# Attention scores of a query tile's two jobs made as one run of matmuls

## The chip, the cores and the metric

One core of a Trainium2 chip runs the whole program. The metric is device microseconds of an execution. TensorE (PE; its weight loads are shown as PEld) makes the matmuls and transposes into PSUM, VectorE (DVE) and ScalarE (ACT) read PSUM and work on SBUF, GpSimd (POOL) works on SBUF, SyncE (SP) issues most DMAs. Each engine runs its own instructions in the order of the program and waits on semaphores.

## The reference

A block of a language model with 1024 tokens: projections, retention, a sparse attention with three branches, two feed-forward layers and a recurrent mixer. The change touches two of the attention's branches, for 8 heads of 64 in 2 key groups:

```python
ss = jnp.einsum('bgrtd,bgtnsd->bgrtns', qb, kb).astype(jnp.float32) * scale
ss = jnp.where(dsel >= 0, ss - sl[..., None, None] * dsel, NEG)
ps = jax.nn.softmax(ss.reshape(B, G, R, T, -1), axis=-1).reshape(ss.shape)      # selected blocks
...
wmask = (dw >= 0) & (dw < WINDOW) & (wpos[None, :] >= 0)
sw = jnp.where(wmask, sw - sl[..., None] * dw.astype(jnp.float32), NEG)
pw = jax.nn.softmax(sw, axis=-1)                                               # the last 512 keys
...
o = gt[0] * o_cmp + gt[1] * o_sel + gt[2] * o_win
```

## The kernel before

The function `nsa_attend` works through 128 jobs, `JOBS = [(h, i, r) ...]`: head h (8), query tile i of 128 tokens (8), and r = 0 for the selected branch, r = 1 for the window. Job j = 2n + r; the two jobs of one (h, i) are a pair, number n. The selected job of tile i has i + 1 key tiles of 128 (causal; what isn't selected is masked by rows that stand with the keys), the window job at most 5.

A job goes through five steps, each on one engine:

- scores (PE): for each run of up to 512 keys a matmul of the queries' low part with the keys and mask rows (`q_low`, 82 rows, `ks_blk` or `kw_blk`), one of the high part with both parts of the keys (`q_high`, `ks_both` or `kw_both`), accumulating in the PSUM tile `sc0` or `sc1` (one for each r, 1024 columns); then a matmul with `eye` and `edges` that adds the causal mask to the last tile, and for window jobs with 5 tiles one for the first tile. The last one counts up `scores_done{r}`.
- maxima (DVE, L2237) and exp with the row sum (ACT, L2220), which writes `att_prob{r}` and counts up `exp_done{r}`. From here the PSUM tile is free for the next pair's scores of the same r.
- weight (DVE, L2246 to L2251): reciprocal of the sum, times the gate, and the scaling of `att_prob`.
- turns (PE, L2170): a transpose for each key tile, into `pt0` or `pt1` in groups of up to 4 tiles; groups with even numbers are copied to SBUF by ACT (L2227), odd ones by DVE (L2273).
- values (PE, L2187): the products with the values, both jobs of a pair into one PSUM tile; the selected job's step begins with two matmuls (L2183) that add the earlier branch's output. After the window job's values, output (DVE, L2261 and L2262) splits the sum into two parts.

The order is written out by hand, one loop over j on each engine. PE: scores(0), scores(1), then for each j scores(j + 2), turns(j), values(j - 1). DVE: for each j weight(j + 1), maxima(j + 2), the odd copies of job j, output(j - 1), which does nothing unless j - 1 is a window job. ACT: for each j the even copies of job j, then exp(j + 2). So scores(j + 2) wait for exp(j), the job of the same r one pair before.

POOL splits each head's queries into `q_high` and `q_low` (L1997 to L1999, four operations), for heads 2 to 7 as soon as the last scores of the head before the last are done, that is, while the last tile of one head and the first of the next are worked on.

Of the kernel before, what the change touches and what calls it, by code (L numbers as in the profile page):

```python
# [6 lines left out]
P = 128  # L7
# [10 lines left out]
HALF = 512  # L18
# [11 lines left out]
NSA_H, NSA_G, NSA_D = 8, 2, 64  # L30
# [3 lines left out]
N_KROWS = N_BLK + 2  # L34
WINDOW = 512
# [2039 lines left out]
def nsa_attend(nc, mem, env, N, projT, selT, ocmp, then, ins):  # L2075
# [8 lines left out]
    qh, q_high, q_low = N["qh"], N["q_high"], N["q_low"]  # L2084
# [7 lines left out]
    JOBS = [(h, i, r) for h in range(NSA_H) for i in range(NT) for r in range(2)]  # L2092
    NJ, PER_HEAD = len(JOBS), 2 * NT
    first = lambda i, r: 0 if r == 0 else max(0, i - WINDOW // P)
    tiles = lambda i, r: i + 1 - first(i, r)
# [8 lines left out]
    with phase(nc, names, banks) as (block, s, ps):  # L2104
        def groups_of(j, parity=None):
            return [n for n in range(before[j], before[j + 1]) if parity is None or n % 2 == parity]

        @block.sync
        def _(sp):
            sp.dma_start(raw, then).then_inc(s["weight_loaded"], 16)  # L2110
            for h in range(1, NSA_H):
                p, b = divmod(h, 2)
                before_it = p - 1 + b
                if before_it > 0:
                    sp.wait_ge(s[f"q_split{b}"], before_it)
                load_queries(nc, sp, qh[b], projT, selT, ins, h, s[f"q_in{b}"])
                if h == 1:
                    for i in range(NT):
                        sp.dma_start(N["o"][:, i, :], ocmp[:, i, :]).then_inc(s[f"o_in{i}"], 16)
# [19 lines left out]

        @block.tensor  # L2140
        def _(pe):
            def scores(j):
                h, i, r = JOBS[j]
                p, b = divmod(h, 2)
                if i == 0 and h > 0:
                    pe.wait_ge(s[f"q_split{b}"], p + b)
                pe.wait_ge(s[f"exp_done{r}"], j // 2)
                n, f, rows = tiles(i, r) * P, first(i, r) * P, NSA_D + N_KROWS
                both_parts, high = (N["ks_both"], N["ks_blk"]) if r == 0 else (N["kw_both"], N["kw_blk"])
                q = slice(i * P, (i + 1) * P)  # L2150
                for c in range(0, n, HALF):
                    w = min(HALF, n - c)
                    out, k = ps[f"sc{r}"][:, c:c + w], slice(f + c, f + c + w)
                    edge, diagonal = n > WINDOW and r == 1 and c == 0, c + w == n
                    nc.tensor.matmul(out, q_low[b][0:rows, q], high[0:rows, p // 2, k], start=True, stop=False, skip_group_check=True)
                    last = nc.tensor.matmul(out, q_high[b][:, q], both_parts[:, p // 2, k], start=False, stop=not (edge or diagonal), skip_group_check=True)
                    if edge:
                        last = nc.tensor.matmul(out[:, 0:P], N["eye"][:], N["edges"][:, P:2 * P], start=False, stop=True, skip_group_check=True)
                    if diagonal:
                        last = nc.tensor.matmul(out[:, w - P:w], N["eye"][:], N["edges"][:, 0:P], start=False, stop=True, skip_group_check=True)  # L2160
                last.then_inc(s[f"scores_done{r}"], 1)

            def turns(j):
                r = JOBS[j][2]
                pe.wait_ge(s[f"scaled{r}"], j // 2 + 1)
                for n in groups_of(j):
                    _, t0, nt = GROUPS[n]
                    pe.wait_ge(s[f"group_copied{n % 2}"], n // 2)
                    for t in range(nt):
                        last = nc.tensor.transpose(ps[f"pt{n % 2}"][:, t * P:(t + 1) * P], prob[r][:, (t0 + t) * P:(t0 + t + 1) * P], ident[:])  # L2170
                    last.then_inc(s[f"grouped{n % 2}"], 1)

            def values(j):
                h, i, r = JOBS[j]
                p, b = divmod(h, 2)
                for n in groups_of(j):
                    pe.wait_ge(s[f"group_copied{n % 2}"], n // 2 + 1)
                out = ps[f"ob{i % 2}"][b * NSA_D:(b + 1) * NSA_D, 0:P]
                if r == 0:
                    if h == 0:  # L2180
                        pe.wait_ge(s[f"o_in{i}"], 16)
                    pe.wait_ge(s[f"o_read{i % 2}"], h * (NT // 2) + i // 2)
                    nc.tensor.matmul(out, N["o"][:, i, h * NSA_D:(h + 1) * NSA_D], ident[:], start=True, stop=False)  # L2183
                v = N["vs"] if r == 0 else N["vw"]
                cols = slice(p // 2 * NSA_D, (p // 2 + 1) * NSA_D)
                for t in range(tiles(i, r)):
                    last = nc.tensor.matmul(out, v[:, first(i, r) + t, cols], probT[r][:, t, :],  # L2187
                                            start=False, stop=(r == 1 and t == tiles(i, r) - 1))
                last.then_inc(s[f"o_done{r}"], 1)

            scores(0)
            scores(1)
            for j in range(NJ):
                if j + 2 < NJ:
                    scores(j + 2)
                turns(j)
                if j > 0:
                    values(j - 1)
            values(NJ - 1)
# [1555 lines left out]
```

## Time and profile before

| | |
|---|---|
| median of 3 runs | 3888.74 us (3884.55 to 3891.54) |
| the profiled execution | 3891.31 us, its span 3889.5 us |
| mean granted TensorE clock | 0.943 of full speed |
| busy: PE, PEld, DVE, ACT, POOL | 90%, 74%, 46%, 22%, 27% of the span |
| attention stage (`nsa_attend`) | 917.9 us (first scores) to 1288.5 us (first matmul of the next stage): 371 us |

Busy shares are means over stages with different limits. The times of the trace count from the start of the span; 1.8 us of the profiled execution lie outside of it.

### The profile page before, as it was taken

Reading aid. Unit: us, or ns where it says so; the run is one execution under the profiler, and the core shown is the slowest. Engines: PE = TensorE matmul, PEld = TensorE weight load, DVE = VectorE, ACT = ScalarE, POOL = GpSimd, SP = SyncE. Lnnn points to the kernel's source line nnn. Section 1 sums busy time; section 2 is a strip of 40 time slices with the busy share of each in tenths; the row PEclk is TensorE's granted clock in tenths of the full one; section 3 lists DMA queues with packets and bytes.
Section 4 is the critical chain, followed back from the end, with each engine's and each line's share of the span. In section 5 each row is a group of like instructions: output and inputs, shape, how many; then the busy total and the mean of one; then the engine's idle time right before and its main releaser. Section 6 shows DMA issues by size and latency. Waiting matters only on the chain. (4 is left out here: it accounts for less than half of the span.)

```text
span 3889.5 us, 55742 instructions
## 1 busy us (share of the span) xinstructions
PE 3510.9 (90%) x23201; PEld 2896.4 (74%) x23201; DVE 1777.2 (46%) x2725; ACT 868.9 (22%) x1258; POOL 1032.2 (27%) x491
## 2 busy tenths in 40 slices
PE   5999999988989889999999789688874889999997
PEld 4878777767777777888888678577763778888886
DVE  4752555324777635555555535144433322323233
ACT  2012122122334212111111220244322131111112
POOL 3333333333110333212212144132202332222121
PEclk7999999999999999999999899889886999999998
DMA  3353433342000312322222164200002111111111
GB/s 97 130 177 115 124 102 109 103 123 81 8 5 1 128 44 76 119 87 73 88 70 81 44 168 120 82 19 34 5 3 94 51 50 40 58 38 59 38 49 44
DMA packets 309559, 285.55 MB, mean 73 GB/s; under 512 B 21326, under 2 KB 276864, under 8 KB 308408
## 3 DMA queue, kind: packets, MB, share of 16 engines
q1 hardware_dynamic: 283882, 209.82, 18.3%
q10 hardware_dynamic: 25186, 72.62, 5.0%
q8 instruction: 153, 2.51, 0.3%
q0 software_dynamic: 288, 0.20, 0.0%
q14 instruction: 50, 0.41, 0.0%
HBM read 221.64 MB, written 60.95 MB: 73 GB/s over the span
## 5 line engine op out<-in xcount | busy, mean ns | idle before, releaser
L710 POOL TENSOR_TENSOR ffn_wlo<-ffn_raw,ffn_whi 128x1024 fp32r<-128x1024 f32 x88 | 211.4, 2404 | 1067.7 <-ACT ffn_whi L898 1011.8
L203 PE MATMUL up<-h_hi,ffn_whi 128*128 128x512 f32 x1408 | 439.0, 393 | 22.0 <-POOL h_lo L404 22.0
L203 PE MATMUL up<-h_lo,ffn_whi 128*128 128x512 f32 x1408 | 435.5, 391 | 0.0
L203 PE MATMUL up<-h_hi,ffn_wlo 128*128 128x512 f32 x1408 | 434.8, 390 | 0.0
L192 POOL TENSOR_TENSOR whi<-raw,ones 128x1024 fp32r<-128x1024 f32 (+1 forms) x87 | 159.2, 1830 | 800.3 <-PE acc L1406 452.0
L203 PEld LDWEIGHTS up<-h_hi,ffn_whi 128*128 128x128 f32 x1408 | 263.1, 189 | 80.1 <-POOL h_lo L404 15.6
L203 PEld LDWEIGHTS up<-h_lo,ffn_whi 128*128 128x128 f32 x1408 | 265.3, 188 | 56.1
L203 PEld LDWEIGHTS up<-h_hi,ffn_wlo 128*128 128x128 f32 x1408 | 265.1, 188 | 55.9
L1406 PE MATMUL acc<-h_hi,whi 128*128 128x512 f32 x816 | 270.7, 413 | 8.7 <-POOL h_lo L404 8.7
L801 DVE TENSOR_TENSOR ffn_prod<-ffn_act,up 128x1024 f32<-128x1024 f32 x44 | 53.7, 1222 | 464.5 <-PE up L203 459.8
L1406 PE MATMUL acc<-h_lo,whi 128*128 128x512 f32 x816 | 255.4, 395 | 0.0
L1406 PE MATMUL acc<-h_hi,wlo 128*128 128x512 f32 x816 | 253.1, 391 | 0.0
L898 ACT ACTIVATE ffn_whi<-ffn_raw 128x1024 fp32r<-128x1024 f32 x84 | 89.1, 1061 | 632.4 <-PE up L203 581.9
L203 PE MATMUL dn<-ffn_ghi,ffn_dhi 128*128 128x512 f32 x704 | 219.0, 392 | 7.9 <-issue 3.9
L203 PE MATMUL dn<-ffn_glo,ffn_dhi 128*128 128x512 f32 x704 | 218.1, 391 | 0.0
L203 PE MATMUL dn<-ffn_ghi,ffn_dlo 128*128 128x512 f32 x704 | 218.1, 391 | 0.0
L1406 PEld LDWEIGHTS acc<-h_lo,whi 128*128 128x128 f32 x816 | 154.9, 190 | 33.9
L1406 PEld LDWEIGHTS acc<-h_hi,wlo 128*128 128x128 f32 x816 | 154.5, 189 | 34.3
L1406 PEld LDWEIGHTS acc<-h_hi,whi 128*128 128x128 f32 x816 | 148.7, 191 | 39.2 <-issue 6.4
L832 DVE SCALAR_TENSOR_TENSOR xT<-dn,prm,xT 128x1024 f32<-128x1024 f32 x88 | 113.0, 1284 | 124.0 <-PE dn L203 124.0
L808 DVE TENSOR_TENSOR ffn_glo<-ffn_prod,ffn_ghi 128x1024 fp32r<-128x1024 f32 x44 | 139.5, 3171 | 56.7 <-ACT ffn_ghi L922 56.7
L830 DVE TENSOR_TENSOR xT<-xT,dn 128x1024 f32<-128x1024 f32 x88 | 107.4, 1221 | 121.8 <-PE dn L203 121.8
(543 smaller groups left out, 6618.5 us busy)
## 6 DMA issues: line engine op xcount, KB each, us to landing
raw<-w_in SPq DMA_DIRECT2D x51, 512.0 KB
projT<-proj_stage ACTq DMA_DIRECT2D x51, 512.0 KB, 2.7
ffn_ada_raw<-w_ada SPq DMA_DIRECT2D x24, 1024.0 KB, 5.0
ffn_raw<-w_up SPq DMA_DIRECT2D x44, 512.0 KB
ffn_draw<-w_down SPq DMA_DIRECT2D x11, 1024.0 KB, 6.7
ffn_raw<-ffn_w_gate SPq DMA_DIRECT2D x22, 512.0 KB
ffn_raw<-ffn_w_up SPq DMA_DIRECT2D x22, 512.0 KB
ffn_draw<-ffn_w_down SPq DMA_DIRECT2D x11, 1024.0 KB, 4.8
```

Of the source, the lines that this page charges most:

```text
L192: return nc.gpsimd.tensor_tensor(out, x, one.unsqueeze(2).broadcast_to(x.shape), ALU.mult)
L203: last = nc.tensor.matmul(acc[:, t, :], w[:, k, w_cols], x[:, k, t * HALF:(t + 1) * HALF], start=(k == 0 and i == 0), stop=(k == k_tiles - ...
L710: nc.gpsimd.tensor_tensor(w_lo[i][:], raw[i][:], w_hi[i][:], ALU.subtract).then_inc(s[f"up_split{i}"], 1)
L801: nc.vector.tensor_tensor(prod[j][:].rearrange("p (h t) -> p h t", h=NH), act_out[:].rearrange("p (h t) -> p h t", h=NH), acc[1][:], ALU.m ...
L808: nc.vector.tensor_tensor(g_lo[:, j, :], prod[j][:], g_hi[:, j, :], ALU.subtract).then_inc(s["g_split"], 1)
L830: nc.vector.tensor_tensor(x, x, dn[b][:], ALU.add).then_inc(s[f"down_read{b}"], 1)
L832: nc.vector.scalar_tensor_tensor(out=x, in0=dn[b][:], scalar=prm[:, gate + n:gate + n + 1], in1=x, op0=ALU.mult, op1=ALU.add).then_inc(s[f ...
L898: nc.scalar.activation(w_hi[i][:], raw[i][:], ACT.Copy).then_inc(s[f"up_hi{i}"], 1)
L1406: last = nc.tensor.matmul(acc[b][:, t, :], w[:, k, :], x[:, k, t * HALF:(t + 1) * HALF], start=(k == 0 and i == 0), stop=(k == KD - 1 and ...
```

## The change

`scores` takes a pair n instead of a job. It waits for the exps of both jobs of pair n - 1, then issues the low part's matmuls for all keys of both jobs, then the high part's, then all masks; the last mask of each job still counts up its `scores_done{r}`. In the loop over j it is called for even j only, ahead of turns(j), for the pair j / 2 + 1, where before scores(j + 2) stood ahead of each turns(j). The matmuls are the same ones, in number and size. DVE's, ACT's and POOL's programs are unchanged.

```diff
--- before.py
+++ after.py
@@ -2139,26 +2139,34 @@
 
         @block.tensor
         def _(pe):
-            def scores(j):
-                h, i, r = JOBS[j]
+            def scores(n):
+
+                h, i, _ = JOBS[2 * n]
                 p, b = divmod(h, 2)
                 if i == 0 and h > 0:
                     pe.wait_ge(s[f"q_split{b}"], p + b)
-                pe.wait_ge(s[f"exp_done{r}"], j // 2)
-                n, f, rows = tiles(i, r) * P, first(i, r) * P, NSA_D + N_KROWS
-                both_parts, high = (N["ks_both"], N["ks_blk"]) if r == 0 else (N["kw_both"], N["kw_blk"])
-                q = slice(i * P, (i + 1) * P)
-                for c in range(0, n, HALF):
-                    w = min(HALF, n - c)
-                    out, k = ps[f"sc{r}"][:, c:c + w], slice(f + c, f + c + w)
-                    edge, diagonal = n > WINDOW and r == 1 and c == 0, c + w == n
-                    nc.tensor.matmul(out, q_low[b][0:rows, q], high[0:rows, p // 2, k], start=True, stop=False, skip_group_check=True)
-                    last = nc.tensor.matmul(out, q_high[b][:, q], both_parts[:, p // 2, k], start=False, stop=not (edge or diagonal), skip_group_check=True)
-                    if edge:
-                        last = nc.tensor.matmul(out[:, 0:P], N["eye"][:], N["edges"][:, P:2 * P], start=False, stop=True, skip_group_check=True)
-                    if diagonal:
-                        last = nc.tensor.matmul(out[:, w - P:w], N["eye"][:], N["edges"][:, 0:P], start=False, stop=True, skip_group_check=True)
-                last.then_inc(s[f"scores_done{r}"], 1)
+                for r in range(2):
+                    pe.wait_ge(s[f"exp_done{r}"], n)
+                q, rows = slice(i * P, (i + 1) * P), NSA_D + N_KROWS
+                spans = [(r, c, min(HALF, tiles(i, r) * P - c)) for r in range(2) for c in range(0, tiles(i, r) * P, HALF)]
+                keys = lambda r, c, w: slice(first(i, r) * P + c, first(i, r) * P + c + w)
+                edge = lambda r, c: r == 1 and c == 0 and tiles(i, r) * P > WINDOW
+                diagonal = lambda r, c, w: c + w == tiles(i, r) * P
+                for r, c, w in spans:
+                    blk = N["ks_blk"] if r == 0 else N["kw_blk"]
+                    nc.tensor.matmul(ps[f"sc{r}"][:, c:c + w], q_low[b][0:rows, q], blk[0:rows, p // 2, keys(r, c, w)],
+                                     start=True, stop=False, skip_group_check=True)
+                for r, c, w in spans:
+                    both_parts = N["ks_both"] if r == 0 else N["kw_both"]
+                    nc.tensor.matmul(ps[f"sc{r}"][:, c:c + w], q_high[b][:, q], both_parts[:, p // 2, keys(r, c, w)],
+                                     start=False, stop=not (edge(r, c) or diagonal(r, c, w)), skip_group_check=True)
+                for r, c, w in spans:
+                    out = ps[f"sc{r}"][:, c:c + w]
+                    if edge(r, c):
+                        nc.tensor.matmul(out[:, 0:P], N["eye"][:], N["edges"][:, P:2 * P], start=False, stop=True, skip_group_check=True)
+                    if diagonal(r, c, w):
+                        nc.tensor.matmul(out[:, w - P:w], N["eye"][:], N["edges"][:, 0:P], start=False, stop=True, skip_group_check=True)\
+                            .then_inc(s[f"scores_done{r}"], 1)
 
             def turns(j):
                 r = JOBS[j][2]
@@ -2189,10 +2197,9 @@
                 last.then_inc(s[f"o_done{r}"], 1)
 
             scores(0)
-            scores(1)
             for j in range(NJ):
-                if j + 2 < NJ:
-                    scores(j + 2)
+                if j % 2 == 0 and j + 2 < NJ:
+                    scores(j // 2 + 1)
                 turns(j)
                 if j > 0:
                     values(j - 1)
```

## Rows read from the trace of the kernel before

**Rows 1.** The page, part 1: busy us, share of the span, instructions.
```profile
PE 3510.9 (90%) x23201; PEld 2896.4 (74%) x23201; DVE 1777.2 (46%) x2725; ACT 868.9 (22%) x1258; POOL 1032.2 (27%) x491
```

**Rows 2.** Windows: busy time of each engine (instructions), granted clock, the attention stage.
```profile
910.00:1290.00 380.00, 341.23 (x2275) 277.16 (x2274) 290.35 (x737) 150.32 (x354) 60.41 (x30) 0.96 0.05 15
```

**Rows 3.** Waits within the attention stage: total us, times, longest us.
```profile
ACT att_prob L2220 <- DVE att_small L2237: 185.0, 116, 4.4
```

**Rows 4.** Timeline of PE, heads 6 and 7: start us, us.
```profile
1232.80 0.50 PE L2155 MATMUL sc<-nsa_ks_blk,att_q_low 82*128 82x512 f32 x1
...
1239.53 0.33 PE L2155 MATMUL sc<-nsa_ks_blk,att_q_low 82*128 82x128 f32 x1
...
1239.91 1.06 PE L2170 MATMUL pt<-ident,att_prob 128*128 128x128 f32 x8
...
1240.90 1.31 PE L2187 MATMUL ob<-att_probT,nsa_vw 128*64 128x128 f32 x10
...
1243.19 0.43 PE L2183 MATMUL ob<-ident,nsa_o 128*64 128x128 f32 x2
...
1245.30 0.39 PE L2155 MATMUL sc<-nsa_ks_blk,att_q_low 82*128 82x256 f32 x1
...
1255.93 0.50 PE L2155 MATMUL sc<-nsa_ks_blk,att_q_low 82*128 82x512 f32 x1
...
1273.93 0.50 PE L2155 MATMUL sc<-nsa_ks_blk,att_q_low 82*128 82x512 f32 x1
...
1274.27 0.39 PE L2156 MATMUL sc<-nsa_ks_both,att_q_high 128*128 128x512 f32 x1
...
1274.50 0.40 PE L2155 MATMUL sc<-nsa_ks_blk,att_q_low 82*128 82x512 f32 x1
...
1275.03 0.93 PE L2170 MATMUL pt<-ident,att_prob 128*128 128x128 f32 x7
```

**Rows 5.** Timeline of DVE and ACT, last pairs of head 7.
```profile
1276.15 1.22 DVE L2237 TENSOR_REDUCE att_small<-sc 128x1 f32<-128x1024 f32 x1
...
1277.40 1.12 ACT L2220 ACTIVATE att_prob<-sc,att_small 128x1024 f32<-128x1024 f32 x1 [1.14 <-DVE att_small L2237]
...
1278.64 0.16 DVE L2246 RECIPROCAL att_small<-att_small 128x1 f32<-128x1 f32 x1 [0.15 <-ACT att_prob L2220]
...
1279.81 0.82 DVE L2237 TENSOR_REDUCE att_small<-sc 128x1 f32<-128x640 f32 x1
...
1280.67 0.80 ACT L2220 ACTIVATE att_prob<-sc,att_small 128x640 f32<-128x640 f32 x1 [1.32 <-DVE att_small L2237]
...
1281.59 0.16 DVE L2246 RECIPROCAL att_small<-att_small 128x1 f32<-128x1 f32 x1 [0.76 <-ACT att_prob L2220]
```

**Rows 6.** Groups by shape, attention stage: busy us, mean ns.
```profile
L2262 DVE TENSOR_TENSOR h_lo<-ob,h_hi 64x128 fp32r<-64x128 f32 x63 | 18.2, 288 | 2.2
...
L2237 DVE TENSOR_REDUCE att_small<-sc 128x1 f32<-128x128 f32 x16 | 4.6, 286 | 5.4 <-PE sc L2160 5.3
...
L2220 ACT ACTIVATE att_prob<-sc,att_small 128x128 f32<-128x128 f32 x16 | 5.9, 367 | 22.6 <-DVE att_small L2237 22.5
```

**Rows 7.** Timeline of DVE while POOL splits queries.
```profile
1190.66 1.47 DVE L2248 TENSOR_TENSOR att_small<-att_small,nsa_gates 128x1 f32<-128x1 f32 x1
1192.16 2.46 DVE L2251 TENSOR_SCALAR att_prob<-att_prob,att_small 128x1024 f32<-128x1024 f32 x1
...
1196.63 2.18 DVE L2248 TENSOR_TENSOR att_small<-att_small,nsa_gates 128x1 f32<-128x1 f32 x1
```

**Rows 8.** Windows around a split of the queries, and one in the next tiles.
```profile
1104.00:1107.00 3.00, 1.65 (x14) 1.34 (x13) 2.95 (x4) 0.27 (x1) 2.18 (x1) 1.00 0.00 0
1107.00:1110.00 3.00, 2.86 (x16) 2.50 (x16) 2.44 (x10) 1.51 (x5) 0.00 (x0) 0.68 0.38 112
...
1211.12:1213.06 1.94, 1.63 (x11) 0.96 (x10) 1.47 (x5) 1.05 (x3) 0.00 (x0) 1.00 0.03 8
```

## The prediction

> **What bounds the kernel now.** I read the page first: TensorE (PE) is busy 90% of the span [rows 1]. That is an average over many stages, so the next view is the busy time of the attention stage alone, the only stage that the diff touches: in 380 us PE is busy 341, VectorE (DVE) 290, ScalarE (ACT) 150 [rows 2]. PE leads, DVE is not far behind. The view of waits shows what to fear: ACT's 116 waits for DVE's maxima sum to 185 us [rows 3]. They cost nothing as long as PE has other work at that time.
>
> The timeline of the last head shows whether it has [rows 4]. Let k be the number of key tiles of the selected job of a pair (tile i has k = i + 1); the window job has min(k, 5). From one pair's first score matmul to the next pair's: i = 0 takes 5.77 us, i = 1 to 3 together 10.63, i = 4 to 6 together 18.00, i = 7 takes 6.73. One head with no disturbance: 41.1 us. In the large pairs PE runs without a gap but for 0.17 us where it takes up a new piece of work. The latency chain (scores, maximum, exp, weighting, transposes) is there too, but the two jobs of a pair run half a pair apart, so one job's chain lies under the other's matmuls.
>
> **PE's prices** [rows 4]. 8 transposes 0.99 us (1239.91 to 1240.90), so T(k) = 0.11 + 0.11k. A values step of the selected job, V0, takes 2.11 us with 8 tiles (1243.19 to 1245.30; 18 matmuls with the two that add the earlier output): 0.17 for taking it up plus 0.108 for each matmul. So one of a window job with 5 tiles, V1, has 10 matmuls and takes 1.24. The selected job's scores of i = 7 take 1.10 (1273.93 to 1275.03): the first start is 0.34 before the next, then 0.23 for every 512 columns, and 0.11 for 128, so 0.11 at the start is fill.
>
> **The chain's prices** [rows 5, 6]. M0 of 1024 columns to exp 1.25, exp with its accumulator to the reciprocal 1.24, W0 (reciprocal, gate, scaling) 1.17, M1 of 640 0.86, its exp 0.92. For 128 columns: maximum 0.29, exp 0.37 against 1.12. I take the sizes between on a straight line. The two output operations take 0.29 each, 0.62 with the gap.
>
> **What the change removes.** Nothing of the matmuls: each still has its own weight load, only their order differs. Saved is one start a pair: 0.17 for the wait and 0.11 for the fill, 0.28 us; 64 pairs, 18 us if PE stays the bound. To the path it is part of S below. The page counts 23201 weight loads for 23201 matmuls [rows 1], though every projection multiplies one weight tile with two halves in succession: grouping equal weights has saved no load in this kernel. The Trainium skill (TensorE: Matmul & The Clock Gate, "Step-by-step: what each phase is for") says that the separate load lets one load serve many matmuls, and that loads are pulled under the running matmul; if one load served a whole group here, the change would be worth more than a start. That is a rival below.
>
> **What it adds: two waits move together.** A pair's scores (both) now wait for both exps of the pair before, and stand in PE's queue ahead of turns(2n), whose input has long been ready. exp of job 2n+1 needs its maximum, which DVE makes only after weight(2n), behind the copy of 2n's transposes and output(2n-1). output(2n-1) needs values(2n-1), which PE makes after the scores and turns(2n). So a loop closes, through all three engines, once a pair:
> scores S, then turns(2n) T, values(2n-1) V1, output 0.11 + 0.62, W0, M1, E1, 0.10 back to PE. The side branch A = M0 + E0 (E0 also behind ACT's copy of the turns) takes the place of B = T + V1 + 0.73 where it is longer. And S is longer than before: the selected job's diagonal mask, which frees its maximum, now comes at the pair's end, at S instead of after about 1.1 of 2.0 us.
>
> **The walk**, for i = 7: S = six 512-column matmuls x 0.23 + five of 128 x 0.11 + 0.11 = 2.04. B = 0.87 (7 tiles) + 1.24 + 0.73 = 2.84; A = 1.25 + 1.24 = 2.49, so B. W0 1.17; M1 + E1 + hand-over 0.82 + 0.04 + 0.89 + 0.13 = 1.88. Sum 7.93 against 6.73. PE's own work in that loop is 2.04 + 0.87 + 1.24 + 0.66 + 1.89 = 6.7, so it would idle 1.2.
> The same for the others (S + the longer of A and B + W0 + M1,E1): i = 6: 1.94 + 2.73 + 1.10 + 1.88 = 7.65; i = 5: 1.82 + 2.41 + 1.03 + 1.88 = 7.14; i = 4: 1.80 + 2.18 (A, behind ACT's copy) + 0.95 + 1.88 = 6.81; together 21.60 against 18.00. i = 3: 1.25 + 1.90 + 0.90 + 1.63 = 5.68; i = 2: 1.04 + 1.56 + 0.83 + 1.39 = 4.82; i = 1: 0.81 + 2.18 (V1 of five tiles from the head before) + 0.76 + 1.16 = 4.91; together 15.41 against 10.63. i = 0: the chain gives 5.27, PE's own work 0.71 + 0.98 + 1.24 + 0.66 + 2.13 + 0.1 = 5.85, which decides, against 5.77.
> A head: 5.85 + 15.41 + 21.60 + 7.93 = 50.8 against 41.1, +9.7 us; eight heads, **+77 us**.
>
> **The splits of the queries.** In six of the eight heads POOL splits the next queries while DVE works, and of weight(j), which takes 1.17 us in all at 1024 columns [rows 5], the gate product then took 1.47 and 2.18 and the scaling 2.46 [rows 7]. Those heads are some 5 us longer. The change moves these DVE operations against POOL's four, by one or two of its 2 us steps: W0 would wait for two of them, about +2.7, and W1 hardly; but PE's longer idle time makes a clock dip likelier there. I price the difference at nothing, bounds -2 and +2 us a head, 12 in all to either side.
>
> **The clock.** In the split of another head, PE was busy 1.65 of 3 us at clock 1.00, in the 3 us after it the granted clock was 0.68 [rows 8], that is, part of it at 1.2 instead of 2.4 GHz. By my walk PE is busy 3.06 of 4.91 us in i = 1, 2.83 of 4.82 in i = 2, 3.7 of 5.68 in i = 3: 59 to 65%, close to that 55%. At half clock i = 2 would have S + 1.04 and turns and values + 0.5: + 1.5 us, once or twice a head if at all, 0 to 3 us a head. I take 1 us a head, 8 in all.
>
> Sum against the profiled execution's own 3891.3: + 77 + 8 = 3976. The median of the runs shown is 2.6 lower, so the forecast for the median is **3974 us**, 2.2% slower.
>
> **Rivals.**
> PE stays the bound (other side: faster). For this, the chain would have to fit in PE's own time, 6.7 us for i = 7, that is, lose 1.2 of my 7.93, and 1.7 in i = 2. If so, only the saved starts count: -18 us, 3871. Were weight loads shared too, 128-column matmuls could go from 0.11 to 0.06 (a quarter of 0.23); about six a pair x 0.05 = 0.3, -37 us in all, 3852. For it: PE is the busiest engine. Against: the chain's parts are each in the rows, and their order is the program's. Chance 6%.
> The chain is shorter than I walk it (turns and values overlap W0 or DVE's order costs less): the loss is a third to two thirds, +20 to +50, about 3925. It decides where output(2n-1) is ready before M0 ends; then A takes the place of B everywhere, -0.35 to -0.5 in i = 5 to 7. That alone is only -11 us, so more would have to be off. Chance 12%.
> The clock falls in every head and stays down in i = 1 to 3, or in large pairs too, where PE would be busy 85%: +5 us a head instead of 1, +117 or more, 4006 upwards. For it: the dips after the splits. Against: a window busy 1.63 of 1.94 us in this stage stood at clock 1.00 [rows 8]. Chance 14%.
> Neither gain nor loss (the chain's loss just meets the saved starts): 2%, no mechanism of its own.
> The forecast, 3945 to 4000: 66%.
>
> **Range and chances.** The forecast's own bounds are +77 with -12 and +12 for the splits, 0 to 24 for the clock, some 15 for the straight lines: 3945 to 4000. Taking in part of the shorter chain below and of the fallen clock above gives 3938 to 4012. A change under 0.2% (8 us) can't be told from none. Slower 0.92, same 0.02, faster 0.06.
>
> **What the profile after would show.** Score matmuls of both jobs in one run of some 2 us for i = 7, ended by three masks; weight loads still one to a matmul, 190 ns. PE idle once a pair until the ACT exp of the window job, 1.2 us in large pairs, 1.5 to 2 in i = 1 to 3; the waits of PE on ACT rise from nearly nothing to 60 to 80 us. DVE's maximum of the selected job waits for the masks. Pair periods for i = 7, 6, 2: 7.9, 7.7, 4.8 us. The stage takes 450 instead of 371 us, all others keep their time. Wrong would be: periods near 6.3 us with no PE idle time (the chain fits), DVE ahead of PE in its order, or a granted clock well under 0.9 in the stage (then the third rival).

## The result and the profile after

The changed kernel takes 3953.74 us (3951.8 to 3960.84), the kernel before 3887.26 in the same comparison: ratio 1.0168, 95% interval 1.0152 to 1.0183, 66 us slower. The forecast was 3974, the range 3938 to 4012.

The profiled execution took 3952.54 us, its span 3950.6. The page's first part and the window of the attention stage, against [rows 1, 2]:

```profile
PE 3521.6 (89%) x23201; PEld 2906.5 (74%) x23201; DVE 1768.1 (45%) x2725; ACT 869.3 (22%) x1258; POOL 1031.0 (26%) x491
```

```profile
910.00:1360.00 450.00, 352.44 (x2289) 291.12 (x2287) 283.22 (x737) 150.65 (x354) 60.28 (x30) 0.91 0.05 14
```

The matmuls and weight loads are 23201 as before. The stage now lasts from 922.8 to 1361.0 us, 438.2 instead of 370.6: +67.6. All other stages together differ by 6.5 us the other way (3512.4 against 3518.9), a difference of single executions. PE's mean clock in the window is 0.91 instead of 0.96, and PE is busy 352 of its 450 us; in the window of the kernel before it was 341 of 380.

The waits of the stage up to 1352 us, that is, without its last nine, against [rows 3]:

```profile
ACT att_prob L2227 <- DVE att_small L2244: 112.5, 63, 4.2
...
PE sc L2157 <- ACT att_prob L2227: 89.6, 56, 3.8
...
DVE h_hi L2268 <- PE ob L2195: 47.2, 61, 1.6
```

ACT waits less for DVE's maxima (112.5 us instead of 185.0), but PE now waits for ACT's exps, 89.6 us in 56 waits, and DVE for the values that its output needs. Waits that cost nothing became waits of the bounding engine.

The loop that the prediction walks is in the timeline, here from the first scores of i = 6 in the last head to those of i = 7, against [rows 4, 5]:

```profile
1338.84 0.64 PE L2157 MATMUL sc<-nsa_ks_blk,att_q_low 82*128 82x512 f32 x2 [1.48 <-ACT att_prob L2227]
...
1340.37 0.28 PE L2168 MATMUL sc<-nsa_edges,nsa_eye 128*128 128x128 f32 x1
...
1340.69 1.09 DVE L2244 TENSOR_REDUCE att_small<-sc 128x1 f32<-128x896 f32 x1 [1.01 <-PE sc L2168]
...
1340.71 0.84 PE L2178 MATMUL pt<-ident,att_prob 128*128 128x128 f32 x6
...
1341.48 1.31 PE L2195 MATMUL ob<-att_probT,nsa_vw 128*64 128x128 f32 x10
...
1342.82 0.29 DVE L2268 CAST h_hi<-ob 64x128 fp32r<-64x128 f32 x1 [0.71 <-PE ob L2195]
1343.15 0.29 DVE L2269 TENSOR_TENSOR h_lo<-ob,h_hi 64x128 fp32r<-64x128 f32 x1
...
1343.48 0.16 DVE L2253 RECIPROCAL att_small<-att_small 128x1 f32<-128x1 f32 x1
...
1344.59 0.82 DVE L2244 TENSOR_REDUCE att_small<-sc 128x1 f32<-128x640 f32 x1
...
1345.45 0.79 ACT L2227 ACTIVATE att_prob<-sc,att_small 128x640 f32<-128x640 f32 x1 [1.44 <-DVE att_small L2244]
...
1346.14 0.19 ACT L2227 ACTIVATION_READ_ACCUMULATOR att_prob<-sc,att_small 128x1 f32 x1
...
1346.48 0.70 PE L2157 MATMUL sc<-nsa_ks_blk,att_q_low 82*128 82x512 f32 x2 [1.32 <-ACT att_prob L2227]
```

Read it down: scores from 1338.84, the selected job's mask at 1340.37, after the low and high parts of both jobs; DVE's maximum at 1340.69. Turns at 1340.71 although their input is older; values of the window job before at 1341.48; output at 1342.82 and 1343.15, and only then W0 (its reciprocal at 1343.48), though exp had its accumulator read by 1342.95. M1 at 1344.59, exp at 1345.45, accumulator at 1346.14, the next scores at 1346.48: 7.64 us, forecast 7.65. PE waited 1.32 of them.

### The profile page after: what moved, and what is told of

The parts are those of the page before. It is cut to its first block and busy times, and to the rows that moved or that the text cites. A ratio compares the mean times of both kernels' runs of the same rounds, so it can differ in the third digit from the quotient of the medians.

```text
span 3950.6 us, 55792 instructions
## 1 busy us (share of the span) xinstructions
PE 3521.6 (89%) x23201; PEld 2906.5 (74%) x23201; DVE 1768.1 (45%) x2725; ACT 869.3 (22%) x1258; POOL 1031.0 (26%) x491
```

## The experiments

"Head" below is the sum of the eight tile periods, from one selected job's first score matmul to the next one's. An "undisturbed" head is the last one, at whose start POOL splits nothing; i = 7, which has no end there, is taken from the sixth head. In the kernels with a closed loop the first, third, fifth and seventh heads are somewhat quicker in i = 1 to 7 than the others (by 1.0 us a head with the joint wait alone, by 0.7 with the call's place alone and with the window maximum ahead of W0, by 1.1 in the changed kernel, by 0.1 in the kernel before), so eight times the undisturbed head is 3 to 4 us too much there.

**Grouping alone.** The kernel before, each single job's matmuls grouped by part:

```diff
-                for c in range(0, n, HALF):
-                    (low, high, masks of this run of keys)
+                for c, w in spans: (low)
+                for c, w in spans: (high)
+                for c, w in spans: (masks)
```

> The kernel before, with the low parts, then the high parts, then the masks of each single job together; calls and waits as before. Theory (the loss comes from the waits that moved, the grouping of equal weights saves no load): no change, 3887 within 8 us, weight loads still 23201. Rival (the order of the matmuls in itself costs or gives, by shared loads or by masks that come late): 10 us or more to either side.

Measured 3889.25 against 3891.64, ratio 0.9995 (0.9982 to 1.0007). The order of the matmuls is worth nothing within the noise; the profile still has 23201 weight loads.

**The joint wait alone.** The kernel before with

```diff
                 pe.wait_ge(s[f"exp_done{r}"], j // 2)
+                if r == 0:
+                    pe.wait_ge(s["exp_done1"], j // 2)
```

> The kernel before, with one wait more: the selected job's scores of the next pair also wait for the window job's exp of this pair. Order of the matmuls and places of the calls as before. Theory (the joint wait closes a loop through scores, turns, values, output, weighting, maximum and exp): by the same walk with S0 alone in the loop, 7.0 us for i = 7, 4.3 for i = 2, 45.4 a head against 41.1, so +34 us, about 3921; PE idles before the selected scores. Rival (the wait is covered by PE's other work, the loss comes from the long run of score matmuls alone): within 8 us of 3887.

Measured 3898.68 against 3891.64, ratio 1.0015 (1.0004 to 1.0026): +7, not +34. Yet the walk is right tile by tile: undisturbed, i = 7 takes 7.00, i = 6 6.69, i = 5 6.21, i = 2 4.23, a head 44.9 against 41.1, or 44.4 as the mean of both sorts of heads, which would be +27. What I had not priced was given back in the heads with a split: they average 46.4, 1.9 us over that mean, where the kernel before pays 5.5 (46.6 over 41.1). Some 3.5 us in each of six heads are the missing 20. DVE's rows at a split show what was held there:

```profile
1200.09 0.16 DVE L2250 TENSOR_TENSOR att_small<-att_small,nsa_gates 128x1 f32<-128x1 f32 x1
1200.28 0.75 DVE L2253 TENSOR_SCALAR att_prob<-att_prob,att_small 128x1024 f32<-128x1024 f32 x1
1201.07 0.82 DVE L2239 TENSOR_REDUCE att_small<-sc 128x1 f32<-128x640 f32 x1
...
1203.04 1.72 DVE L2250 TENSOR_TENSOR att_small<-att_small,nsa_gates 128x1 f32<-128x1 f32 x1
1204.80 2.26 DVE L2253 TENSOR_SCALAR att_prob<-att_prob,att_small 128x640 f32<-128x640 f32 x1
```

The gate product and the scaling of 1024 columns went ahead of POOL's first operation at 1200.40 (0.16 and 0.75 us); only the window job's were held, to 1.72 and 2.26. In [rows 7] three were: 1.47, 2.46 and 2.18. The price of a split is all in i = 0, which takes 7.6 us instead of the undisturbed 5.7, where the kernel before takes 10.2 to 11.8 instead of 5.8. How much of the difference each held operation makes was not separated.

**The place of the call alone.** The kernel before with both scores calls at even j, each with its own wait:

```diff
-                if j + 2 < NJ:
+                if j % 2 == 0 and j + 2 < NJ:
                     scores(j + 2)
+                    scores(j + 3)
```

> The kernel before, with the two jobs' scores called one behind the other at even j, each with its own wait, masks and release as before (the selected maximum is released after its own scores). Theory: the loop closes through the window job's wait, with S1 alone in it: 6.9 us for i = 7, 4.3 for i = 2, 45.6 a head, +36 us, about 3923; the rest of the changed kernel's loss, about 30 us, belongs to the longer S with the masks at its end. Rival (place of the call costs everything): about 3953 as the changed kernel. Rival (only the grouping costs): about 3887.

Measured 3912.74 against 3891.64, ratio 1.0058 (1.0039 to 1.0077): +21, expected +36. An undisturbed head takes 44.3 (walk 45.6), 44.0 as the mean of both sorts, +23 in all; the splits give some 3 back (48.9 a head, 4.9 over). In the times, the wait alone costs a tenth and the place alone a third of what both cost together; in the undisturbed heads they are nearly alike, 3.3 and 2.9 us of the 8.3 that both cost.

**The order inside the pair.** The changed kernel, joint wait and place kept, but each job's low, high and mask matmuls in the order before:

```diff
-                for r, c, w in spans: (low)
-                for r, c, w in spans: (high)
-                for r, c, w in spans: (masks)
+                for r, c, w in spans:
+                    (low, high, masks of this run of keys)
```

> The changed kernel with its joint wait and its place of the call, but inside the pair each job's low, high and mask matmuls in the order before, so that the selected job's scores are released after 1.1 us instead of 2.0 for i = 7. Theory (B, through turns, values and output, is the longer branch, and exp of the selected job stands behind ACT's copy of the turns): no change against the changed kernel, 3946 to 3960. Rival (the masks at the end make the maximum late, and that costs): about 3915 to 3925, near the run with each job's own wait.

Measured 3960.55 against 3888.08, ratio 1.0183 (1.0154 to 1.0213), the changed kernel's 1.0168 within it. The late mask costs nothing that shows, as it must if the branch through turns, values and output is the longer one. The prediction's remark that the selected job's mask comes late was true and without effect; what lengthens the loop is that both jobs' scores stand in it, in whichever order.

**Turns and values ahead of the scores.** The changed kernel with

```diff
-                if j % 2 == 0 and j + 2 < NJ:
-                    scores(j // 2 + 1)
                 turns(j)
                 if j > 0:
                     values(j - 1)
+                if j % 2 == 0 and j + 2 < NJ:
+                    scores(j // 2 + 1)
```

> The changed kernel with turns(j) and values(j - 1) issued ahead of the pair's scores at even j instead of behind them. Theory (turns and values stand in the loop only because the scores, which wait, are ahead of them): they fill PE's idle time, output(2n-1) is done before the selected maximum ends, the side branch A takes the place of B: 0.35 us less for i = 7, about 1.1 for i = 1, 3.4 a head, 27 in all: about 3927. Rival (S, the weighting and M1 with its exp make the loop, turns and values don't matter): within 8 us of 3954.

Measured 3974.35 against 3888.08, ratio 1.0217 (1.0182 to 1.0252): 47 us over my expectation and some 20 over the changed kernel's 3954, whose interval (1.0152 to 1.0183) just touches this one. The theory of this run fell for the large tiles. PE, DVE and ACT at the end of i = 4 in the last head:

```profile
1343.24 0.82 DVE L2244 TENSOR_REDUCE att_small<-sc 128x1 f32<-128x640 f32 x1
1343.26 0.42 PEld L2178 LDWEIGHTS pt<-ident,att_prob 128*128 128x128 f32 x4 [1.13 <-DVE att_prob L2258]
1343.26 0.66 PE L2178 MATMUL pt<-ident,att_prob 128*128 128x128 f32 x4 [0.89 <-DVE att_prob L2258]
1343.98 0.68 DVE L2280 COPY att_probT<-pt 128x512 f32<-128x512 f32 x1
1344.10 0.80 ACT L2227 ACTIVATE att_prob<-sc,att_small 128x640 f32<-128x640 f32 x1 [1.87 <-DVE att_small L2244]
1344.71 0.14 PEld L2178 LDWEIGHTS pt<-ident,att_prob 128*128 128x128 f32 x1 [1.03 <-DVE att_probT L2280]
1344.71 0.33 PE L2178 MATMUL pt<-ident,att_prob 128*128 128x128 f32 x1 [0.80 <-DVE att_probT L2280]
1344.79 0.19 ACT L2227 ACTIVATION_READ_ACCUMULATOR att_prob<-sc,att_small 128x1 f32 x1
...
1344.97 1.97 PE L2195 MATMUL ob<-att_probT,nsa_vw 128*64 128x128 f32 x8
...
1346.87 0.80 PE L2157 MATMUL sc<-nsa_ks_blk,att_q_low 82*128 82x512 f32 x1
```

Turns(2n) can't fill the idle time: they wait for W0 (to 1343.26), and the fifth tile waits for the PSUM group that DVE copies at 1343.98, behind M1; it starts at 1344.71. Values follow at 1344.97, the scores at 1346.87, while exp had been read by 1344.98. (The granted clock fell to 0.50 at 1345, so about half of these 1.9 us is the clock's; at full clock i = 4 takes 7.14 us in the seventh head against 6.56 in the changed kernel.) I had taken turns and values as ready because in the changed kernel they come after the scores, where all this is long over. Ahead of the scores they add their own waits to the loop.

In the small tiles the theory held: i = 1 takes 3.7 to 3.9 us, 0.9 to 1.0 less than in the changed kernel, expected 1.1. In the seventh head i = 4 to 7 lose 0.6, 0.5, 0.5 and 0.8. The largest loss is at a split, where i = 7 takes 11.5 to 13.2 us instead of the changed kernel's 10.5; i = 0 gives 1.7 to 2.7 of it back in most heads.

**The splits.** Both kernels, POOL writing one column instead of each split of heads 2 to 7:

```diff
-                split_queries(nc, steps, mem.one, qh[b], q_high[b], q_low[b]).then_inc(...)
+                if h < 2:
+                    split_queries(nc, steps, mem.one, qh[b], q_high[b], q_low[b]).then_inc(...)
+                else:
+                    nc.gpsimd.tensor_tensor(q_low[b][0:NSA_D, 0:1], qh[b][0:NSA_D, 0:1],
+                                            q_high[b][0:NSA_D, 0:1], ALU.subtract).then_inc(...)
```

> The kernel before without POOL's splits for heads 2 to 7: one column is written in their place, so heads 2 to 7 work with queries of heads 0 and 1 and the output is not the reference's. Every wait and all work on the other engines stay. Theory: the tile after a split takes 10.2 to 11.8 us with POOL's four operations and 5.8 without, 5.5 us a head, six heads: 33 us less, 3855. Rival (the long tile comes from the wait for new queries or from the clock alone): less than 10 us.

> The changed kernel without POOL's splits for heads 2 to 7, left out as in the run before. Theory: the changed kernel pays only 2.9 us for a split (2.8 more in i = 7, 1.6 to 2.6 more in i = 0, one dip of the clock less in i = 3), 17 us in all: 3937, and the distance to the kernel before without splits is the walk's own, 77 to 90 us. Rival (the splits cost both kernels the same and the walk is too long): 3920, a distance of 66.

Before: 3853.49 against 3888.08, ratio 0.9904 (0.9881 to 0.9928), 35 us are the splits'. After: 3939.36, ratio 1.0129 (1.0106 to 1.0152) to the kernel before with its splits; the changed kernel with its splits has 1.0168, so leaving them out gains 0.0039, 15 us. Without splits the two kernels lie 86 us apart. That the 15 us are not the price of the splits alone is seen below, tile by tile.

**The window maximum ahead of W0.** The changed kernel with one edit in DVE's loop:

```diff
+                if j % 2 == 1 and j + 2 < NJ:
+                    maxima(j + 2)
                 if j + 1 < NJ:
                     weight(j + 1)
-                if j + 2 < NJ:
+                if j % 2 == 0 and j + 2 < NJ:
                     maxima(j + 2)
```

> The changed kernel with one edit on DVE: at odd j the window job's maximum stands ahead of the selected job's weighting W0 instead of behind it; output(2n-1) stays ahead of both. Theory: W0 and the exp before it leave the loop, which becomes S + T + V1 + 0.73 + M1 and its exp: 6.8 for i = 7, 3.8 for i = 2, 43.7 a head instead of 50.8, 57 us less, about 3897, and the rest down to the run with both maxima together is the price of output(2n-1) in the loop. Rival (only the order of the two maxima among themselves matters, or output alone): 3930 to 3955.

Measured 3880.41 against 3891.63, ratio 0.9978 (0.9963 to 0.9993). The loop without W0, i = 7 of the sixth head:

```profile
1182.64 0.71 PE L2157 MATMUL sc<-nsa_ks_blk,att_q_low 82*128 82x512 f32 x2 [0.21 <-ACT att_prob L2227]
...
1187.16 0.29 DVE L2269 TENSOR_TENSOR h_lo<-ob,h_hi 64x128 fp32r<-64x128 f32 x1
...
1187.49 0.82 DVE L2244 TENSOR_REDUCE att_small<-sc 128x1 f32<-128x640 f32 x1
...
1188.35 0.80 ACT L2227 ACTIVATE att_prob<-sc,att_small 128x640 f32<-128x640 f32 x1 [0.33 <-DVE att_small L2244]
...
1188.83 2.46 DVE L2258 TENSOR_SCALAR att_prob<-att_prob,att_small 128x1024 f32<-128x1024 f32 x1
...
1189.38 0.30 PE L2157 MATMUL sc<-nsa_ks_blk,att_q_low 82*128 82x128 f32 x1
```

Output at 1187.16, M1 at 1187.49, exp at 1188.35, scores at 1189.38: 6.74 us from 1182.64, expected 6.8; i = 2 3.82 (3.8), an undisturbed head 43.3 (43.7). In these rows the scaling of 1024 columns still takes 2.46 us beside POOL, but nothing in the loop stands behind it: the time is 17 us better than the walk. Heads with a split average 45.1 us here, 2.2 over the undisturbed mean (42.9), where the changed kernel's are 5.0 over; and after the first head the clock never falls.

**Both maxima together.** The changed kernel with both ahead of output and W0:

```diff
-                if j + 2 < NJ:
+                if j % 2 == 0 and j + 2 < NJ:
                     maxima(j + 2)
+                    maxima(j + 3)
```

> The changed kernel with one edit on DVE: the window job's maximum is taken right behind the selected job's, ahead of that job's weighting, as both score tiles are ready together. Theory (what costs is that the window exp stands behind output, weight and maximum in DVE's order): the loop shrinks to scores, two maxima, exp; PE is the bound again with one start less a pair, about 6.5 us for i = 7; the 66 us come back and some 10 to 18 more: 3870 to 3880. Rival (the joint wait itself or the long run of score matmuls costs, whatever DVE's order): still 3920 to 3955.

Measured 3861.88 against 3891.64, ratio 0.9923 (0.9904 to 0.9941): faster than both kernels. The stage and a pair of it, i = 6:

```profile
920.50:1258.00 337.50, 316.64 (x2215) 261.43 (x2216) 279.82 (x731) 145.22 (x352) 60.34 (x30) 0.97 0.05 15
```

```profile
1243.83 0.64 PE L2157 MATMUL sc<-nsa_ks_blk,att_q_low 82*128 82x512 f32 x2
...
1245.66 1.82 DVE L2244 TENSOR_REDUCE att_small<-sc 128x1 f32<-128x896 f32 x2 [0.99 <-PE sc L2168]
...
1248.88 0.79 ACT L2227 ACTIVATE att_prob<-sc,att_small 128x640 f32<-128x640 f32 x1
...
1250.06 0.72 PE L2157 MATMUL sc<-nsa_ks_blk,att_q_low 82*128 82x512 f32 x2
```

DVE makes both maxima from 1245.66, ACT's window exp starts at 1248.88, and the next scores at 1250.06 find PE busy until then: 6.23 us. PE is busy 317 of 338 us at clock 0.97. Tiles i = 3, 4 and 5 gain against before (3.9, 4.9 and 5.7 us for 4.5, 5.6 and 6.15), i = 7 takes the 6.7 that PE's own work needs. What they gain is mostly idle time of PE in the kernel before, 0.42, 0.53 and 0.29 us, in which values or turns waited for DVE's copies; here it is 0.16, 0 and 0. Two of these waits, before:

```profile
1257.95 0.87 PE L2187 MATMUL ob<-att_probT,nsa_vw 128*64 128x128 f32 x6 [0.53 <-DVE att_probT L2273]
...
1263.30 0.33 PE L2170 MATMUL pt<-ident,att_prob 128*128 128x128 f32 x1 [0.29 <-DVE att_probT L2273]
```

So the prediction's "in the large pairs PE runs without a gap" holds for i = 6 and 7 alone, and the 0.28 us a pair that it has the change save with PE as the bound show only in part: PE is busy 0.30 us less in i = 3, 0.12 and 0.19 in i = 4 and 5, 0.04 in i = 6, and as long as before in i = 7. An undisturbed head is 39.6 us, 1.5 under before, twelve in all; each head with a split 42.1, so 2.5 over instead of 5.5, 18 in all: 30.

**The same, with each job's matmuls in turn.** The two edits together:

> The run with both maxima together, and inside the pair each job's matmuls in the order before, so that the selected maximum can start while PE makes the window job's scores. Theory (with DVE's order mended PE is the bound in i = 4 to 7, the small tiles still wait for exp): nothing in the large pairs, up to 0.3 us less in i = 1 to 3, at most 7 us in all: 3855 to 3864. Rival (the grouping of equal weights was worth something once PE is the bound): 3867 or more.

Measured 3862.94 against 3891.63, ratio 0.9916 (0.9891 to 0.9941): no difference to the run before within the noise. With PE as the bound, too, the order inside the pair, and with it the grouping of equal weights, is worth nothing that shows.

## Why the prediction was right, and where its terms were off

The mechanism is right and shown; the forecast of the time was 20 us too high (3974 for 3954), and more than half of that lies in the loop. Here is the sum of the prediction beside what the periods of the profiled executions give. The undisturbed tile periods at full clock are those of the two kernels without splits.

| term, us | forecast | measured |
|---|---|---|
| the loop at full clock | 77 | 66 |
| the splits: the tiles i = 7 and i = 0 around them, clock dips in i = 0 included | 0 (-12 to +12) | -5 (27.8 against 33.0) |
| the clock elsewhere | 8 (0 to 24) | 7 |
| sum | 85 | 68 |

The stage of the profiled executions grew by 67.6. The 7 us of the clock are 2.5 in i = 3 of the heads that begin with a split, 2.1 in the last head and 2.6 in the first, which begins at a granted clock of 0.50 in both kernels and stays there longer in the changed one.

**The loop: the term that was mis-sized.** Its form is right, and shown from several sides: taking W0 out of it gave the periods that the walk then has, taking output out as well gave the whole loss back. At full clock the heads with an even number (second, fourth and so on) take, from i = 7 down to 0, 7.92, 7.63, 7.12, 6.72, 5.51, 4.67, 4.65 and 5.73, read from several heads of the run without splits, as none of its heads is free of clock dips; forecast 7.93, 7.65, 7.14, 6.81, 5.68, 4.82, 4.91 and 5.85 (the walk's own parts for i = 0 add to 5.82). That is 50.0 instead of 50.8. The first, third, fifth and seventh head are quicker in the large tiles (7.64, 7.36, 6.85, 6.56), 48.9 in all; the walk, made from rows of the last head, didn't have this. The mean, 49.4, is 8.3 over before, forecast 9.7. Eight heads, the last without its i = 7, give 66. Of the 11 us too much, 7 are the 0.8 us in every head, mostly its small tiles, 4 are the quicker heads and 1 is the last tile, which has no next scores to delay. The quicker heads' 0.27 us in i = 6 lie on DVE, between output's first operation and M1 (in the last two heads of the changed kernel M1 starts 0.60 us after the scaling does in the seventh and 0.72 in the eighth); why is open.

**The splits.** "I price the difference at nothing, bounds -2 and +2 us a head" was right, and so was the walk to it: "W0 would wait for two of them, about +2.7, and W1 hardly; but PE's longer idle time makes a clock dip likelier there". At each of the six splits i = 7 takes 2.6 to 2.8 us more than without (10.4 to 10.6 for 7.6 to 7.9), and i = 0 1.6 or 2.6 more (7.3 or 8.35 for 5.73) at a granted clock of 0.77 or 0.66; PE has no idle time in i = 0 of the last head, so a lower clock shows there in full. That is 4.6 a head, where the kernel before pays 5.5, all in i = 0. The rows of the changed kernel at a split, against [rows 7]:

```profile
1190.31 1.25 DVE L2255 TENSOR_TENSOR att_small<-att_small,nsa_gates 128x1 f32<-128x1 f32 x1
1191.60 2.46 DVE L2258 TENSOR_SCALAR att_prob<-att_prob,att_small 128x1024 f32<-128x1024 f32 x1
...
1195.94 0.33 DVE L2255 TENSOR_TENSOR att_small<-att_small,nsa_gates 128x1 f32<-128x1 f32 x1
```

Gate product and scaling of the selected job, which stand in the loop, are held as before (1.25 and 2.46 us for 0.16 and 0.75 undisturbed); the window job's gate product, at 1195.94, comes when POOL is at the end of its last operation: 0.33 us instead of 2.18. The Trainium skill (SBUF — State Buffer, "SBUF: two separate sides") has it that of a VectorE operation with two SBUF inputs or in a 2-port mode and a GpSimd operation the one that starts first keeps the other out for the whole instruction; the trace agrees, with the 1.25 us for the gate product and 2.46 for the scaling, and the maximum from PSUM at its usual 0.82 beside POOL (row 1201.07 of the joint wait's run).

**The clock, and what the run without splits shows.** Without splits the two kernels lie 86 us apart. The loop gives 66 of it; the rest is the clock, of which the prediction had 8. The second to the seventh head measured 52.2 us on average against 49.4 at full clock, so about + 22 in eight heads. Each has one or two dips, at i = 2 to 5. One, in the last head of the changed kernel, which has no split at its start either, as windows, against [rows 8]:

```profile
1310.00:1313.00 3.00, 1.47 (x10) 0.97 (x9) 1.99 (x9) 0.56 (x2) 0.00 (x0) 1.00 0.00 0
1313.00:1316.00 3.00, 3.00 (x16) 2.17 (x16) 2.01 (x8) 0.95 (x3) 0.00 (x0) 0.68 0.00 0
1316.00:1319.00 3.00, 2.15 (x7) 1.58 (x7) 1.87 (x6) 0.67 (x2) 0.00 (x0) 0.50 0.00 0
1319.00:1322.00 3.00, 3.00 (x13) 2.15 (x13) 0.90 (x2) 1.16 (x3) 0.00 (x0) 0.50 0.00 0
1322.00:1325.00 3.00, 2.48 (x11) 1.78 (x10) 2.45 (x8) 0.78 (x2) 0.00 (x0) 0.61 0.00 0
1325.00:1328.00 3.00, 3.00 (x21) 2.57 (x21) 1.53 (x4) 0.60 (x2) 0.00 (x0) 1.00 0.00 0
```

With PE busy 1.47 of 3 us the clock was still 1.00; then it fell, and stayed at 0.50 for some ten us in which PE was busy 2.15 to 3.00 of 3 us. i = 3 took 7.32 us there instead of 5.5. In the six heads that begin with a split this dip is nearly gone: i = 1 to 6 of them are 0.4 us a head over full clock, all in i = 3, where the run without splits has 2.8. So leaving the splits out took away 30 us (27.8 at the splits and 2.5 in i = 3) and brought back 17 of clock dips, 13.6 us in all by the periods of these tiles; the times say 15, from ratios whose intervals are some 0.2% (8 us) to either side. That is why the 15 us are no price of the splits, and why the 86 us came so near the 85 of the sum: for the kernels without splits the loop was 11 too high and the clock 14 too low, which is luck.

**The rivals.** "PE stays the bound" fell: PE waits 89.6 us for exps. Shared loads fell twice: 0.9995 for the grouping alone, no difference with PE as the bound. "The chain is shorter than I walk it" (+20 to +50) fell, though it points the right way: the chain was a seventh shorter, not a third. The clock fell in nearly every head, as the third rival has it, but with splits it cost little outside of i = 0, and without them 2.8 us a head instead of its 5. The signs that were named came: one run of scores with masks at its end, loads one to a matmul, PE idle once a pair; the stage grew by 67.6 us where 79 were forecast, and the waits on ACT, forecast 60 to 80, were 90.

**Open.** Where exactly a clock dip begins isn't told by these runs, nor why a split at the start of a head leaves so little of the dip in i = 2 to 5, nor why every other head is quicker. The periods are of one profiled execution each, and the dips lie differently from head to head. The 6.5 us by which the other stages differ in the two profiles were not followed.

## What to carry to other kernels

When a group of work is merged on one engine, look at what order the engines before it give their own work: the merged group waits for the last of its inputs, and whatever stands ahead of that input on any queue joins the loop. Here the merge with the old DVE order cost 66 us, with DVE's two maxima merged as well it gained 30. Turn such a loop into a sum, engine by engine, from one timeline; here it was right within 1.5% in i = 4 to 7 and within 6% in the short ones, for the head it was made from; walk a second head too, as every other one was quicker. And price contention by which of the held operations stand in the loop, not by its length.

## What the runs showed that I had not expected

Leaving out a disturbance doesn't give its price when something else depends on it. The same four POOL operations cost the kernel before 33 us by the periods and 35 by the time. In the changed kernel they cost 28 in the tiles around them, yet leaving them out gained only 15, as the granted clock then fell for longer later in each head. Only the comparison tile by tile shows both parts.

What a split costs depends on where the operations that it holds stand: 5.5 us a head in the kernel before, 1.9 when only a wait was added and the selected job's gate product (0.16 us) and scaling went ahead of POOL, 2.2 when W0 was held for as long as ever (2.46 us) but stood outside the loop. So an added wait cost 7 us in the time where the undisturbed tiles lose 27.

Putting work that seemed ready ahead of a wait made the kernel some 20 us slower, as that work had waits of its own that its old place hid.
